# A four-part edit around the norms, the spare PSUM banks and the last head of a decoder step on one NeuronCore

## What is computed

```
def _rmsnorm(x, g):
    xf = x * rsqrt(mean(x * x) + eps);  return xf * g

def _layer(x, pos, st, lp):
    h = _rmsnorm(x, norm_mix_pre)
    y, new_st = _token_mixers(h, pos, st, lp)   # w_in -> 8 gated-delta, 4 retention, 4 mLSTM heads -> w_out
    x = x + _rmsnorm(y, norm_mix_post)
    h = _rmsnorm(x, norm_mlp_pre)
    u = square(relu(h @ w_up))
    x = x + _rmsnorm(u @ w_down, norm_mlp_post)
```

## Time and profile before

| | us |
|---|---|
| median of 3 runs | 3164.97 (3157.7 to 3167.55) |
| the profiled execution | 3165.47 |
| its span, first to last instruction | 3163.9 |
| PE busy | 3090.7 (98%) |
| DVE busy | 1892.9 (60%) |
| ACT busy | 1572.4 (50%) |
| mean granted TensorE clock | 0.992 |

### The profile page before, as it was taken

One profiled execution on the slowest core, in us unless ns is written; L12 is line 12 of the kernel. 1 busy time (PEld: TensorE's weight loads), 2 busy tenths in 40 slices (PEclk: granted clock), 3 DMA queues, 4 the chain that ended last, 5 costly groups with the idle time before them and its releaser, 6 DMA issues.

```text
span 3163.9 us, 67350 instructions
## 1 busy us (share of the span) xinstructions
PE 3090.7 (98%) x23204; PEld 3026.6 (96%) x23204; DVE 1892.9 (60%) x3914; ACT 1572.4 (50%) x3660; POOL 85.4 (3%) x163
## 2 busy tenths in 40 slices
PE   8999999998999999999999999999989999999997
PEld 7999999898999999999989999998989999999997
DVE  6677776656545545455576777755565455454555
ACT  5477775545334334334445777754454343343343
POOL 1100000000000000000001000000000000000000
PEclk9999999999999999999999999999999999999999
DMA  6544445553454544444445444454534444454444
GB/s 208 174 154 139 143 137 164 154 179 126 165 167 160 167 164 160 167 164 161 150 139 175 145 144 146 141 163 146 170 120 162 167 163 161 162 167 164 164 164 153
DMA packets 267258, 499.98 MB, mean 158 GB/s; under 512 B 34529, under 2 KB 39937, under 8 KB 267073
## 3 DMA queue, kind: packets, MB, share of 16 engines
q1 hardware_dynamic: 244224, 443.64, 43.7%
q0 software_dynamic: 14784, 51.05, 4.7%
q10 hardware_dynamic: 8064, 2.80, 0.3%
HBM read 475.38 MB, written 22.01 MB: 157 GB/s over the span
## 4 chain that ended last, share of the span: by engine, by line
PE 89%; DVE 5%; ACT 3%; DMA 2%; issue 2%; ACTq 0%; DVEq 0%; SPq 0%; POOLq 0%
PE PU L518 78%; PE PABCD L518 5%; PE PF L518 2%; PE PE_ L518 2%; DMA RAW<-in_w 1%; ACT Y L877 1%; DVE WL L1259 1%; PE PABCD L521 1%; ACT WH L877 1%; PE PE_ L521 1%; ACT AE L877 0%; DVE Y L1438 0%; DVE Y L1279 0%; DVE X L1281 0%; DVE HL L1264 0%
## 5 line engine op out<-in xcount | busy, mean ns | idle before, releaser
L518 PE MATMUL PU<-HH,WH 128*128 128x288 f32 x4096 | 1271.9, 311 | 33.0 <-DVE HL L1264 24.2
L877 ACT ACTIVATE WH<-RAW 128x512 fp32r<-128x512 f32 x1669 | 964.4, 620 | 563.9 <-PE PU L518 415.1
L1259 DVE TENSOR_TENSOR WL<-RAW,WH 128x512 fp32r<-128x512 f32 x1668 | 1076.2, 687 | 259.3 <-ACT WH L877 245.3
L518 PE MATMUL PU<-HL,WH 128*128 128x288 f32 x4096 | 1211.5, 296 | 0.0
L518 PE MATMUL PU<-HH,WL 128*128 128x288 f32 x4096 | 1207.8, 295 | 0.0
L518 PEld LDWEIGHTS PU<-HH,WH 128*128 128x128 f32 x4096 | 773.7, 189 | 56.5 <-issue 36.7
L518 PEld LDWEIGHTS PU<-HL,WH 128*128 128x128 f32 x4096 | 774.1, 189 | 5.7
L518 PEld LDWEIGHTS PU<-HH,WL 128*128 128x128 f32 x4096 | 774.0, 189 | 0.0
L518 PE MATMUL PU<-UH,WH 128*128 128x288 f32 x2560 | 760.2, 297 | 3.1 <-DVE UL L1429 1.9
L518 PE MATMUL PU<-UL,WH 128*128 128x288 f32 x2560 | 755.9, 295 | 0.0
L518 PE MATMUL PU<-UH,WL 128*128 128x288 f32 x2560 | 753.4, 294 | 0.0
(11 more groups left out here) (254 smaller groups left out, 2191.5 us busy)
## 6 DMA issues: line engine op xcount, KB each, us to landing
RAW<-in_w SPq DMA_DIRECT2D x1669, 256.0 KB, 3.8
SIN<-in_sin POOLq DMA_DIRECT2D x32, 512.0 KB, 4.9
out_sout<-Y POOLq DMA_DIRECT2D x32, 512.0 KB, 5.5
BC<-gate_rows POOLq DMA_DIRECT2D x32, 304.0 KB, 4.4
AUX<-in_aux POOLq DMA_DIRECT2D x32, 152.0 KB, 3.3
X<-in_x SPq DMA_DIRECT2D x4, 576.0 KB, 8.9
out_y<-X SPq DMA_DIRECT2D x8, 288.0 KB, 2.1
out_sout<-SOUT ACTq DMA_DIRECT2D x32, 64.0 KB, 2.4
```

What stands on the lines that cost most here:

```text
L518: return nc.tensor.matmul(out, lhsT, rhs, start=start, stop=stop, skip_group_check=True)
L877: return nc.scalar.activation(out, in_, f, **kw)
L1259: tt(WL[s % 2][:, k], RAW[c][:], WH[s % 2][:, k].bitcast(F32), ALU.subtract).then_inc(sem("lo_ready"), 1)
```

## The change

DVE's `update_x` is split into `scale_y` and `add_x`: the scale of a pair now stands ahead of the `HL` pair before it and the add behind, and `HL` of chunks 0 and 1 follows the first update at once. On ACT weight piece 4 is made inside `prenorm`. In the two-at-once quads units 2 and 3 get the banks `PE_` and `PF`, and the evacuations of units 0 and 1 move to slot 15, behind the pieces 8 to 11. Norm sums use 32 columns of the ones and write partition quarter `c % 4`; ACT copies the result to `S`, PE folds the quarters with a 128x128 matrix of ones (slot 17, or slot 9 in layer 0's first quad), and the logarithm divides by 32 times as much. The last head multiplies each sample's state directly with its four columns into `PF` at slot 6.

```
+        def bank(kind, l, s):
+
+            return (PE_, PF)[s - 2] if two_at_once(kind, l) and s >= 2 else PU[s % 2]
...
 
                 s, kk = JOINED[t] if joined else SIDE_BY_SIDE[t] if two_at_once(kind, l) else divmod(t, 8)
                 hi, lo = (UH, UL) if kind in ("out", "down", "down0", "down_last") else (HH, HL)
-                if kk == 0:
...
-            def norm_sum(e, c, slot, first=False, last=False):
-
+            def norm_sum(e, c):
+
+                j = c % 4
                 pe.wait_ge(sem("squares"), NC_ * e + c + 1)
-                mm(PC[:, 0:T], ONES[:], SQ[:, slot], first, last).then_inc(sem("squares_summed"), 1)
+                mm(PC[NS * j:NS * j + NS, 0:T], ONES[:, 0:NS], SQ[:, j], c < 4, c >= NC_ - 4).then_inc(sem("squares_summed"), 1)
+
+            def norm_fold(e):
+
+                pe.wait_ge(sem("s_ready_log"), 2 * e + 1)
+                mm(PC[:, 0:T], ONES[:], S[:]).then_inc(sem("squares_summed"), 1)
 
             def norm_part(t, kind, l, x):
 
                 if kind in ("first", "up_first"):
 
-                    for c in chunks_at(t - 1, kind, l) if two_at_once(kind, l) else chunks_at(t, kind, l):
-                        norm_sum(2 * l + (1 if kind == "up_first" else 0), c, c % 4, c == 0, c == NC_ - 1)
+                    e = 2 * l + (1 if kind == "up_first" else 0)
+                    if two_at_once(kind, l):
+                        at, fold = (t if 1 < t < 16 else t - 1 if t == 1 else -1), 17
+                    else:
+                        at, fold = t, 9
+                    for c in chunks_at(at, kind, l):
+                        norm_sum(e, c)
+                    if t == fold:
+                        norm_fold(e)
 
...
+            def linear_read_direct(kind, x):
+                n, nk, hk, par, pair = x
+                pe.wait_ge(sem(f"{kind}_qs"), nk + 1)
+                pe.wait_ge(sem("state_in"), 16 * (n + 1))
+                for b in range(NB):
+                    c = slice(SEQ + DS * b, SEQ + DS * b + DS)
+                    i = mm(PF[:, c], SIN[:, b], SMALL[:, 0, DS * b:DS * b + DS], b == 0, False)
                 i.then_inc(sem("state_read"), 1)
 
...
                 elif kind in ("ret", "mls"):
-                    read, _, select = LAST_READ if last else EARLY_READ if early else LINEAR_READ
-                    if t == read:
+                    if last and t == LAST_SLOTS[3]:
+                        linear_read_direct(kind, x)
+                    read, _, select = EARLY_READ if early else LINEAR_READ
+                    if not last and t == read:
                         linear_read(kind, x)
-                    if t == select:
+                    if not last and t == select:
...
                         fn(SQ[:, c % 4], X[:, c], ACT.Square).then_inc(sem("squares"), 1)
-                    if (e or l) and g in (1, 3, 5):
-                        hi_part(Q, g // 2 + 5)
+                    if (e or l) and g in (0, 1, 3, 5):
+                        hi_part(Q, (g + 1) // 2 + 4)
                 if e == 0 and l == 0:
-                    for piece in range(4, 8):
+                    hi_part(Q, 4)
+                    norm_copy(0)
+                    for piece in range(5, 8):
                         hi_part(Q, piece)
-                norm_scale("squares_summed", NC_ * (2 * l + e // 2 + 1), S, "s_ready")
+                    prenorm_scale(0)
+
+            def norm_copy(e):
+
+                act.wait_ge(sem("squares_summed"), (NC_ + 1) * e + NC_)
+                fn(S[:], PC[:, 0:T]).then_inc(sem("s_ready_log"), 1)
+
+            def prenorm_scale(e):
+                act.wait_ge(sem("squares_summed"), (NC_ + 1) * (e + 1))
+                fn(S[:], PC[:, 0:T], ACT.Ln, scale=1.0 / (NS * D_MODEL), bias=EPSC[:, 0:1]).then_inc(sem("s_ready_log"), 1)
+                act.wait_ge(sem("s_ready_log"), 2 * (e + 1))
+                fn(S[:], S[:], ACT.Exp, scale=-0.5).then_inc(sem("s_ready"), 1)
 
...
                         output_squares(t, kind, l, x)
+                    if two_at_once(kind, l) and t in (8, 14):
+                        e = 2 * l + (1 if kind == "up_first" else 0)
+                        norm_copy(e) if t == 8 else prenorm_scale(e)
+                    if kind == "up_first" and t == 15:
+                        hi_part(Q, 12)
                     for s in (s,) if kind == "up" and c == 7 else {15: (0, 1), 23: (2,), 31: (3,)}.get(t, ()) if kind == "up_first" else ():
 
                         act.wait_ge(sem("up_relu"), up_units(l, x, s) + 1)
                         fn(UPT[s % 2], UPE[s % 2], ACT.Square).then_inc(sem("up_square"), 1)
                     joined = l if last_head else None
+                    if kind == "up_first" and t == 15 or kind in ("out", "down_last") and x[1] == 3 and t == 31:
+                        continue
                     if t % 2 and not (last_head and t == 13) and not (kind in ("first", "up_first") and t < 7):
                         if last_head and t == 15:
                             hi_part(Q, 11, joined)
...
+            def add_x(l, which, g):
+
+                e = 2 * l + which
+                k = slice(2 * g, 2 * g + 2)
                 dve.wait_ge(sem("y_scaled"), 9 * e + g + 2)
                 tt(X[:, k], X[:, k], Y[:, k], ALU.add).then_inc(sem("x_updated"), 2)
 
...
                         gdn_front(t, l, front)
-                    if two_at_once(kind, l) and t in (8, 10):
-                        evac(Q, t // 2 - 4, kind, l, x)
+                    if two_at_once(kind, l) and t == 15:
+                        evac(Q, 0, kind, l, x)
+                        evac(Q, 1, kind, l, x)
                     if t % 8 == 7 and not (last_head and t == 7) and not (two_at_once(kind, l) and t < 16):
                         evac(Q, t // 8, kind, l, x)
                         if kind == "gdn" and t == 31:
...
-                    if kind == "up_first" and t == 15:
+                    if kind == "up_first" and t == 17:
                         store_up(l, x, 0)
                         store_up(l, x, 1)
 
             def update_and_split(l, which, lo_l, lo_which, lo_gain, Q):
 
                 for g in range(8):
-                    update_x(l, which, g)
+                    scale_y(l, which, g)
+                    if g != 1:
+                        prenorm_lo(lo_l, lo_which, lo_gain, range(max(2 * g - 2, 0), max(2 * g, 2)))
                     if g:
-                        prenorm_lo(lo_l, lo_which, lo_gain, range(2 * g - 2, 2 * g))
+                        add_x(l, which, g)
                     if g in (1, 3, 5):
                         lo_part(Q, g // 2 + 4)
...
                     for g in range(8):
-                        update_x(l, 1, g)
+                        scale_y(l, 1, g)
+                        if g > 1:
+                            add_x(l, 1, g - 1)
+                    add_x(l, 1, 7)
                 dve.wait_ge(sem("x_updated"), 2 * (8 + 16 * l + 16))
                 dve.sem_inc(sem("layer_free"), 1)
 
```

More of the change, by code:

```diff
@@ L526, in unit_part @@
                 hi, lo = (UH, UL) if kind in ("out", "down", "down0", "down_last") else (HH, HL)
-                if kk == 0:
+                psum = bank(kind, l, s)[:, 0:T]
+                if kk == 0 and not (two_at_once(kind, l) and s >= 2):
                     pe.wait_ge(sem("psum_read"), 4 * Q + s + 1)
@@ L939, in output_squares, with norm_scale @@
                 fn(Y[:, c], Y[:, c], scale=gain).then_inc(sem("output_squares"), 1)
-            def norm_scale(summed, count, dst, name):
-                act.wait_ge(sem(summed), count)
+            def norm_scale(count, dst, name):
+                act.wait_ge(sem("output_summed"), count)
                 fn(dst[:], PC[:, 0:T], ACT.Ln, scale=1.0 / D_MODEL, bias=EPSC[:, 0:1]).then_inc(sem(f"{name}_log"), 1)
-                act.wait_ge(sem(f"{name}_log"), count // NC_ if summed == "squares_summed" else count)
+                act.wait_ge(sem(f"{name}_log"), count)
                 fn(dst[:], dst[:], ACT.Exp, scale=-0.5).then_inc(sem(name), 1)
@@ L1188, in mixer @@
                 elif kind in ("ret", "mls"):
-                    if t == (LAST_READ if last else EARLY_READ if early else LINEAR_READ)[1]:
+                    if not last and t == (EARLY_READ if early else LINEAR_READ)[1]:
                         act.wait_ge(sem("state_read"), x[0] + 1)
@@ L1265, in prenorm_lo, with scale_y @@
                         .then_inc(sem("hl_ready"), 1)
-            def update_x(l, which, g):
+            def scale_y(l, which, g):
                 e = 2 * l + which
```

20 lines of the change are left out of this document (11 added, 9 removed).

## The result

The changed kernel took 3142.19 us (median of 5 runs, 3141.26 to 3145.37) beside 3161.4 for the kernel before (5 runs): a ratio of 0.9932, interval 0.9919 to 0.9945. On 3161 us that is 21.5 won (17 to 26); the two medians as they stand lie 19.2 apart. The sum said 20.3, between the two. The profiled execution has a span of 3140.6, against 3163.9.

What follows compares the result with a forecast made beforehand. PE, busy 98% of the span, was taken as the bound, with time only in its waits and clock. Terms 6.0 + 4.5 + 4.2 + 3.1 + 1.3 + 1.2 = 20.3 us gave a median of 3144.7, range 3136 to 3155.

Steps and rivals of the forecast that it cites:

- the clock's 3.1: Windows at 2200 and 2338: the waits ahead of them go, so the low clock goes, 1.8 and 1.3 us won.
- "up_first", 3.0 each: Quad at the boundary in both layers: wait of 2.63 before unit 2 mostly goes, 3.0 us won a layer, 6.0 together.
- Slot 1 was put at 1.4: At "up_first", PE starts 1.55 us earlier but loses it in a new 1.4 us wait for weight piece 4.
- I take 0.65: Norm sums of two chunks in two quarters: assumed 0.65 us a pair, between 0.48 (full overlap) and 0.97 (none).
- the predicted wait of 1.8 at slot 13: In "up_first", PE, faster than DVE there, waits some 1.8 us for weight piece 7 instead of 0.27.
- The pair's price: Norm sums of two chunks on PE, by the narrower sums in quarters: 0.31 us saved a pair.
- "first" of layer 1, 4.5: Layer 1's first quad: cheaper norm pairs and no 2.00 wait, less a new 2.3 wait; 4.5 us, 3.7 with low clock.
- Last heads, 2.1 each: Last head of each layer: direct reads replace read, wait and fold, 2.1 us won each, 4.2 for two.
- "first" of layer 0, 1.3: Layer 0's first quad: eight cheaper norm pairs less the fold, with ACT nearly full; 1.3 us won, bounds 0 and 2.0.
- The end, 1.2: End of the program: seven pairs of scale and add by 0.17 us each, 1.2 us won.
- The new waits eat it: Rival, chance 0.13: clock falls behind new waits at slots 1, 13 and 18; 12.6 us won instead of 20.3, 3152.
- Slower by the clock at the boundaries: Rival, chance 0.05: PE's standstill behind slot 1 keeps the clock low, 22 us lost against 20.3 won, 3167.

Runs made afterwards that it cites:

- experiment 4: Changed kernel with norm sums, fold, banks and evacuations as before; only DVE's boundary order and the last heads stay changed: 3158.11 us, ratio 0.9974.
- experiment 2: The kernel before, unchanged, run again for a second profile: 3168.33 us in one execution.
- experiment 6: Changed kernel with both halves of weight piece 4 made earlier, on ACT and DVE: 3139.08 us, ratio 0.9913.
- experiment 10: Changed kernel again, 3147.65 us; with layer 1's first quad rearranged, 3145.29; last, that with weight piece 4 early too, 3141.29.
- experiments 7 and 8: Changed kernel with all norm sums in one quarter, 3161.03 us; changed kernel with layer 0's first quad adding four chunks at once, 3146.49 us.
- Experiment 5: Changed kernel with DVE's order at the boundaries and end, and piece 4 on ACT, as before: 3143.53 us, ratio 0.9933.
- Experiment 9: Changed kernel with layer 1's gates' product at slot 21 instead of 18, DVE's step behind it later too: 3145.16 us, ratio 0.993.
- experiment 1: Changed kernel with the last heads as before (read at slot 4, masked by ACT, folded at slot 6): 3151.89 us, ratio 0.9958.

## Why the prediction came out right, and where its steps did not

The sum, 20.3, is 1.2 below the 21.5 measured, and that it is so near is in part luck, since errors of 2 to 5 us cancelled. By the stretches (means of two profiles each, 22 in all), with the clock's 3.1 given to the places from which it was read:

| place | predicted | measured |
|---|---|---|
| last heads, with 1.8 of clock | 6.0 | 11.3 |
| `"up_first"`, with 1.3 of clock | 7.3 | 7.5 |
| layer 1's first quad | 4.5 | 2.4 |
| layer 0's first quad | 1.3 | 0 to 0.8 |
| the end | 1.2 | 1.3 |

*"up_first", 3.0 each.* The two profiles of each kernel give 3.4 and 4.1, the rows 29.1 - 26.06 - 0.48 = 2.5 up to where unit 2 goes on. The mechanism was as told: 2.6 us of wait gone, shown by experiment 4, and the early start lost at slot 1. The rest, 0.9 and 1.6, is mostly the clock, which fell behind that wait in two of four places (experiment 2) and from which the prediction had taken 1.3, in layer 1. Slot 1 was put at 1.4 and is 1.04 to 1.24. Two steps inside were wrong and cancelled: "I take 0.65" for a norm pair is 0.79, and the predicted wait of 1.8 at slot 13 doesn't exist in the changed kernel. PE comes too late for it, because its pace is 2.39 a pair (DVE's 2.22) and because the hole and the low clock behind it hold PE back. Without the hole the wait is there: 0.52 in the second `"up_first"` of experiment 6, 1.05 and 1.36 in the last kernel of experiment 10.

*The pair's price* is a term mis-sized: 0.18 won a pair, not 0.31. It lies between the bounds 0.48 and 0.97 because of full overlap, 0.48, and 0.31 for the change of shape (experiments 7 and 8). The kernel before could have told it. The 0.73 for the gates is measured from their start to the second product behind them, but they start 0.22 behind the product ahead, where products start 0.13 apart. The row ahead of the group at 27.02 is

```profile
26.80 0.29 PE L518 MATMUL PU<-HH,WL 128*128 128x288 f32 x1
```

With that 0.09 a group of gates costs 0.82, and a pair of norm sums, which has the same row (0.68), 0.79. The Trainium skill (TensorEngine Tiling (Array Packing), Key Properties) says that a change of tiling mode drains the engine; the 0.31 is in keeping with it, though no row shows a drain as such.

*"first" of layer 1, 4.5.* This is the step that failed: 2.4 by the stretches. The prediction let the early start and the new wait at slot 1 cancel to nothing and said no more of them; the clock at that place it kept for a rival. Experiment 5 shows what they cost: with DVE's old order, no early start and no hole, the same quad wins 4.6. So the banks and the norm sums brought what was forecast, and the order took some 2 us of it, by a clock that stayed at the lower level for 8.2 and 8.9 us behind PE's start in place of 2.9. (The 4.6 is from one profile, and experiment 5 moves ACT's half of piece 4 as well.) Inside the sum, eight pairs at 0.79 win 1.0 less than was summed; the new wait was foreseen at 2.3 and is 2.15, and the clock fell behind it, which the prediction had as its lower value (3.7) and did not take. The rotation, which hangs on DVE's chain, stands 49.7 us behind PE's start before and after in the first profiles (51.2 and 49.9 in the second). That doesn't make PE's earlier start the gain: experiment 4 has that start and a stretch of 179.3, experiment 5 has not and is at 174.1. Experiment 9 shows that the rotation hangs on unit 2's end: behind the first scale, unit 2's evacuation stands at 38.9 and the rotation at 50.2, against 40.8 and 52.1 in the changed kernel, 1.9 sooner each.

*Last heads, 2.1 each.* 2.4 each from the transposes to step 3 (8.05 before, 5.62 now), in part since 16 reads take 1.70, not 1.9. Under-sized was the clock: 1.8 in layer 1 only, where the low clock cost some 2 to 3.5 in each layer (experiment 2). The two heads won 11.3 together by the stretches of the profiles, beside 6.0; putting them back costs 4.5 by the profile of experiment 1, in which the clock stayed up, and 8 (2 to 14) by its ratio. The surplus of some 5 us is what made up for the two first quads.

*"first" of layer 0, 1.3.* The gates' product stands at 36.59 against 37.36, so 0.8, but at 37.16 against 37.18 in the second profiles: what it won is not shown. *The end, 1.2.* 1.27.

*The order at the boundaries* had no term of its own, but its early start was the reason for the slot 1 wait. Experiments 4 and 5 show that it won nothing at the boundaries as made, and experiment 6 that it won 0.7 to 1.5 us a boundary (92.2, 172.6 and 92.2 against 93.5, 174.1 and 93.0, one profile each) once piece 4 was out of its way.

*The rivals.* "The new waits eat it" was half true in place (the clock fell behind `z`) and not in sum. "Slower by the clock at the boundaries" named the right mechanism, and it was at work: slot 1 starts 2.8 us behind PE's start, and the clock came back 6.0 to 9.1 behind it, so 3.2 to 6.3 beyond slot 1, where the rival needed 7 or more.

What stays open: why the clock fell behind all four waits for `RHS` in the kernel before and behind neither in experiment 1, when behind equal waits ahead of unit 2 it fell in two of four; how much of the 8 us of experiment 1 comes of the clock in its executions that weren't profiled (their mean granted clock is 0.991 to 0.992, that of the changed kernel's 0.993 to 0.994, which fits with some, but shows no place); and the 2.2 us by which the heads' stretches differ between executions of one kernel.

## What to carry to other kernels

A wait that is removed gives back its length and, where the clock had fallen behind it, about as much again (here 2.4 for the path of a last head, and some 2 to 3.5 for the clock). Since the clock falls behind some waits and not behind others, one profile doesn't price it: take a second before building on it. A start that is made earlier and followed by a hole gives back nothing, or less (2 us lost in layer 1's first quad), so look for what the second slot needs before moving the first. Price an operation of unknown overlap from both sides, read its cost from the product ahead of it to the products behind it, and then ask which engine sets the pace at each price. Work that an in-order engine has to do before a chain begins belongs in the idle time in which it waits for that chain's first input.

## What the runs showed of the hardware

- Sums with 32 stationary columns over 288 moving ones: two chunks in two quarters of a bank 0.79 us of PE's time, in one quarter 1.27, with all columns 0.97. Four chunks in four quarters have rows of 0.69, two in two have 0.68.
- A 128x128 stationary operand with four moving columns costs 0.106 us an instruction (16 in 1.70 us), nearly as much as with 32 columns (0.12).
- Behind waits of 2.2 to 3.0 us, PE's granted clock fell to 0.50 in some cases and not in others. For one and the same wait of 2.63 us, ahead of unit 2 of `"up_first"`, it fell in two of four.
- At a boundary the clock was at the lower level for 2.9 to 6.0 us behind PE's start where PE went on without a hole (kernel before, experiments 5 and 6), and for 6.0 to 9.1 us in the changed kernel, where PE stood still for 1.04 to 1.24 us behind the first slot.
